# Differential queries and keys as three products of rounded halves, on one core

## The reference, cut to what matters

```python
xn = _rms(x, norm_mix_g)
z = jnp.einsum('btd,dc->btc', xn, w_in)
(m_qk, m_v, m_o, m_if, s_q, s_ckv, i_q, i_k, i_w, d_q, d_k, d_v, g_pre) = _split_cols(z)
...
y_b = _dsa(sq, sk, sv, iq, ik, i_w).reshape(B, T, S_WIDTH)
dq = _rope(_rms(d_q.reshape(B, T, DA_HEADS, 2, DA_HEAD_DIM), dq_g), cos, sin)
dk = _rope(_rms(d_k.reshape(B, T, DA_HEADS, 2, DA_HEAD_DIM), dk_g), cos, sin)
...
o = _diff_attn(dq, dk, dv, lam_val)
...
merged = (gates[:, :, 0] * jnp.einsum('btc,cd->btd', y_a, w_branch[0]) + ...
x = x + jnp.einsum('btd,de->bte', merged, w_out)
```

## Time and profile before

| | us |
|---|---|
| median of three runs | 2467.02 (2466.3 to 2468.4) |
| the profiled execution | 2466.4 |
| its span, first to last instruction | 2464.6 |
| TensorE busy | 2441.3 (99% of the span) |
| VectorE busy | 1851.7 (75%) |
| ScalarE busy | 1552.4 (63%) |

### The profile page before, as it was taken

How to read it: one execution, slowest core, us unless ns; L and a number is a source line. 1 busy time by engine, 2 the same in 40 slices (tenths; PEclk the granted TensorE clock), 3 DMA queues, 4 the chain that set the end, 5 groups by cost and what they waited for, 6 DMA issues and landing times.

```text
span 2464.6 us, 30527 instructions
## 1 busy us (share of the span) xinstructions
PE 2441.3 (99%) x12038; PEld 2037.7 (83%) x12038; DVE 1851.7 (75%) x1866; ACT 1552.4 (63%) x1896; POOL 111.3 (5%) x78
## 2 busy tenths in 40 slices
PE   9999999999999999999999999999999999999998
PEld 8788888897888888977888897888888888888886
DVE  7877744478786446645454479999999999999998
ACT  5666543367565444365443447788878787878886
POOL 0000000000000000010000002010101010101001
PEclk9999999999999999999999999999999999999999
DMA  7444555354336565677654556999999999999996
GB/s 260 145 154 154 208 190 181 117 186 153 132 137 212 199 212 171 204 258 261 250 188 176 166 197 265 395 369 380 374 373 380 373 377 367 381 366 390 358 383 249
DMA packets 185399, 634.31 MB, mean 257 GB/s; under 512 B 14324, under 2 KB 55668, under 8 KB 142089
## 3 DMA queue, kind: packets, MB, share of 16 engines
q1 hardware_dynamic: 175688, 608.21, 67.6%
q0 software_dynamic: 9536, 23.60, 2.5%
HBM read 616.56 MB, written 26.22 MB: 261 GB/s over the span
## 4 chain that ended last, share of the span: by engine, by line
PE 95%; DVE 3%; ACT 1%; issue 0%; DMA 0%; DVEq 0%; SPq 0%; ACTq 0%
PE bank L565 92%; PE bank L602 2%; PE bank L935 2%; DVE split L2210 1%; ACT split L1562 0%; DVE parts L2190 0%; PE bank L1483 0%; ACT parts L1562 0%; DVE oT_high L2224 0%; DVE x_resid L2252 0%; DMA const<-in_tables 0%; DVE xparts L2190 0%; DVE parts L2279 0%; DVE merged_low L2242 0%; DVE xs L2936 0%
## 5 line engine op out<-in xcount | busy, mean ns | idle before, releaser
L565 PE MATMUL bank<-split,parts 128*128 128x512 f32 (+1 forms) x6432 | 1465.7, 388 | 6.2 <-DVE split L2210 2.2
L565 PEld LDWEIGHTS bank<-split,parts 128*128 128x128 f32 x6432 | 1186.9, 188 | 251.7 <-issue 12.2
L1562 ACT ACTIVATE split<-ring 128x2048 fp32r<-128x2048 f32 x444 | 848.6, 1921 | 438.5 <-PE bank L565 437.8
L2210 DVE TENSOR_TENSOR split<-ring,split 128x2048 fp32r<-128x2048 f32 x444 | 993.7, 2284 | 45.8 <-ACT split L1562 45.5
L2279 DVE TENSOR_TENSOR parts<-bank,parts 128x512 fp32r<-128x512 f32 x128 | 82.5, 686 | 166.5 <-ACT parts L1562 165.8
L1562 ACT ACTIVATE halves<-ring 128x1024 fp32r<-128x1024 f32 x96 | 101.0, 1060 | 130.0 <-PE bank L565 129.6
L2224 DVE TENSOR_TENSOR halves<-ring,halves 128x1024 fp32r<-128x1024 f32 x96 | 116.2, 1224 | 73.0 <-ACT halves L1562 72.3
L565 PE MATMUL bank<-ring_low,z_high 128*128 128x512 f32 (+2 forms) x384 | 147.0, 383 | 0.0
L565 PE MATMUL bank<-xparts,halves 128*128 128x256 f32 x960 | 116.5, 283 | 0.2 <-DVE x_resid L2252 0.2
L565 PEld LDWEIGHTS bank<-xparts,halves 128*128 128x128 f32 x960 | 115.5, 192 | 0.8 <-DVE x_resid L2252 0.6
L565 PE MATMUL bank<-z_high 128*128 128x512 f32 (+3 forms) x304 | 111.2, 366 | 0.0
(11 more groups left out here) (349 smaller groups left out, 2411.9 us busy)
## 6 DMA issues: line engine op xcount, KB each, us to landing
ring<-in_moe_w_gate SPq DMA_DIRECT2D x112, 1024.0 KB, 7.7
ring<-in_moe_w_up SPq DMA_DIRECT2D x112, 1024.0 KB, 7.4
ring<-in_moe_w_down SPq DMA_DIRECT2D x112, 1024.0 KB, 7.6
ring<-in_w_gate_up SPq DMA_DIRECT2D x44, 1024.0 KB, 5.9
ring<-in_w_in SPq DMA_DIRECT2D x40, 1024.0 KB, 5.3
ring<-in_ret_w_in SPq DMA_DIRECT2D x24, 1024.0 KB, 5.3
ring<-in_w_down SPq DMA_DIRECT2D x22, 1024.0 KB, 6.8
ring<-in_w_in SPq DMA_DIRECT2D x20, 880.0 KB, 4.7
```

Of the source, the lines that this page charges most:

```text
L565: return nc.tensor.matmul(o, l, r, start=first, stop=final, **kw)
L1562: return nc.scalar.activation(out, in_, func, **kw)
L2210: V.tensor_tensor(split[:, split_place(m), 1, :], ring[:, n % RING, :], split[:, split_place(m), 0, :].bitcast(F32), ALU.subtract).then_in ...
```

## The change

In both layers of the first block:

- `dq` and `dk` are computed by `split_chunk`: their units get high parts (places B, A1 and A2, B) and low parts, and three rounded products take the place of one float32 product.
- In `split_chunk`, a unit that is not computed tile by tile starts when its high part is there: first the products with the weights' high part for both tiles (16), then a wait for the low part and the products with it (8).
- The inputs' second low part `xnT_low` and its signal are gone; all chunks use `xs_low`. `xnT` is free early, and `kv` and the merged branches live there; two places of the late half units swap.
- TensorE's order is `dq`, `dk`, the first unit of `dv`, the turning of the heads, the second unit of `dv`, the selected scores.
- ScalarE's and VectorE's orders are written anew around this: three of the new low parts stand inside `top_keys`, and the selected scores come after the rotation of the differential queries.

```diff
-COLUMNS = {"qk": "A1 A2", ... "kv": "A2", "dv": "A1 A2",
+COLUMNS = {"qk": "A1 A2", ... "kv": "A2", "dq": "B A1", "dk": "A2 B",
+           "dv": "A1 A2",
...
-            xnT_low = oT_high[:, KT:2 * KT, :].rearrange("p (t k) s -> p t k s", t=TT)
...
-        kv = xs
+        kv = xnT[:, :, :].rearrange("p (s k) t -> p s (k t)", s=TT)
+        merged = kv
...
+            def with_high(o, l, r, first):
+
+                mm(o, l(0), r(0), first, False)
+                mm(o, l(1), r(0), False, False)
+
+            def with_low(o, l, r, final):
+
+                return mm(o, l(0), r(1), False, final)
...
-                    w = take_column((4, n), chunk)
+                    w = take_column((4, n), chunk, column_low if u in by_tile else column_high)
+                    low = len(unit_of_column)
                     ins = []
-                    for tt in range(TT):
+                    if u not in by_tile:
+                        for part in range(2):
+                            if part:
+                                eng.wait_ge(column_low.sem, low)
+                            for tt in range(TT):
+                                c = slice(tt * P, (tt + 1) * P)
+                                for k in range(4 * u, 4 * u + 4):
+                                    l, r = (lambda i: mix_part(i, k)[:, c]), (lambda i: row(w[i], k % 4))
+                                    if part:
+                                        ins.append(with_low(bank[b[tt]][:, 0:n], l, r, k == KT - 1))
+                                    else:
+                                        with_high(bank[b[tt]][:, 0:n], l, r, k == 0 and bias is None)
+                    for tt in range(TT if u in by_tile else 0):
...
                 columns(z_dq, "dq")
-                tiles_dk = chunk_tiles(z_dk[1])
-                next(tiles_dk)
+                columns(z_dk, "dk")
+                units_dv = split_chunk(z_dv[1], "dv")
+                next(units_dv)
                 turn_heads(lambda tt, c: zc(tt, C_SQ + c, P), lambda tt, c: kv[:, tt, c:c + P])
...
-                next(tiles_dk)
-                next(tiles_dk, None)
-                point("dk")
+                for _ in units_dv:
+                    pass
+                point("dv")
                 head_scores(0)
...
-                eng.wait_ge(gate_in_low.sem, pe.next(gate_in_low))
-                low_in[0] = xnT_low
-                columns(z_dv, "dv")
...
+                column_highs("dq0")
                 z_evac(*z_o, ACT.Sigmoid)
-                column_highs("dv0")
+                column_highs("dq1")
                 for tt in range(TT):
                     for h in range(2):
                         copy(kv[:, tt, h * HALF:(h + 1) * HALF])
+                column_highs("dk0")
                 head_squares(lambda tt, h: kv[:, tt, h * HD:(h + 1) * HD], 8, lambda tt: kB + 8 * tt, in_yb)
+                column_highs("dk1")
+                z_evac(*z_dq)
+                column_highs("dv0")
                 roots(hsum[:, 2, kB:kY], hsum[:, 1, kB:kY])
+                head_squares(z_head(C_DQ), 8, lambda tt: kA + 25 * tt + 8, in_yb)
                 column_highs("dv1")
-                z_evac(*z_dq)
-                head_squares(z_head(C_DQ), 8, lambda tt: kA + 25 * tt + 8, in_yb)
+                z_evac(*z_dk)
+                head_squares(z_head(C_DK), 8, lambda tt: kA + 25 * tt + 16, in_yb)
+                turned_heads(0)
                 head_roots(8, 16)
-                z_tile(0, *z_dk)
-                turned_heads(0)
-                z_tile(1, *z_dk)
-                exps({2: ("g10",), 5: ("g11",)})
-                head_squares(z_head(C_DK), 8, lambda tt: kA + 25 * tt + 16, in_yb)
+                column_highs("g10")
                 z_evac(*z_dv)
+                exps({0: ("g11",)})
                 column_highs("g12")
...
-                column_lows("v0", "v1")
+                column_lows("v0", "v1", "o0")
                 head_mean_squares(z_heads(1, 0, 8), z_heads(0, 0, 8), HD)
-                column_lows("o0")
...
-                top_keys()
+                top_keys({(1, 0): ("dq0",), (1, 3): ("dq1",), (1, 6): ("dk0",)})
                 eng.wait_ge(act_freed.sem, dve.point("kv", act_freed))
                 V.memset(v_ext[:, :, :, M_DH:M_DH + 1], 1.0)
                 head_mean_squares(hsum[:, 1, kB:kY], hsum[:, 0, kB:kY], HD)
+                column_lows("dk1")
                 then(inverse_root(hsum, slice(kB, kY)))
                 for tt in range(TT):
+                    if tt:
+                        column_lows("dv0")
                     rope(kv[:, tt, 0:HALF], 8, tt, hsum[:, 3, kB + 8 * tt:kB + 8 * tt + 8], 1, done=rope_dve if tt else None)
-                column_lows("dv0", "dv1")
+                column_lows("dv1")
                 head_mean_squares(z_heads(1, 8, 16), z_heads(0, 8, 16), HD)
-                eng.wait_ge(for_act.sem, dve.point("dk", act_freed))
-                V.tensor_tensor(xnT_low, xnT[:, :, :].rearrange("p (t k) s -> p t k s", t=TT), xs_high.bitcast(F32),
-                                ALU.subtract).then_inc(gate_in_low.sem, gate_in_low.tick())
-                scores(lambda tt: msel[:, 0:P] if tt == 0 else msel[:, P:384])
-                column_lows("g10", "g11")
                 z_inverse(8, 16)
                 rope_from_z(C_DQ, 1)
+                column_lows("g10")
+                scores(lambda tt: msel[:, 0:P] if tt == 0 else msel[:, P:384], {2: ("g11",)})
                 head_mean_squares(z_heads(1, 16, 24), z_heads(0, 16, 24), HD)
```

More of the change, by code:

```diff
@@ L46 @@
 LAYER_HALVES = DEPTH * KT
-COLUMNS = {"qk": "A1 A2", "ckv": "B Y", "ix": "A1 A2", "sq": "B Y", "v": "A1 A2", "o": "B A1", "kv": "A2", "dv": "A1 A2",
+COLUMNS = {"qk": "A1 A2", "ckv": "B Y", "ix": "A1 A2", "sq": "B Y", "v": "A1 A2", "o": "B A1", "kv": "A2", "dq": "B A1", "dk": "A2 B",
+           "dv": "A1 A2",
            "g1": "E H A2 E", "b1": "A2 E", "g0": "H D A2 H", "g2": "A2 D E H", "b0": "G D", "b2": "H B"}
@@ L210, in build @@
             split = fx("split", [P, SPLITS, 2, UNIT])
-        late_halves = [oT_high[:, KT:2 * KT, :].rearrange("p k t -> p (k t)"), ybuf_tmp_high[:, 0:UNIT],
+        late_halves = [oT_high[:, 0:KT, :].rearrange("p k t -> p (k t)"), ybuf_tmp_high[:, 0:UNIT],
                        ybuf_tmp_high[:, 3 * 4 * SEQ:3 * 4 * SEQ + UNIT],
-                       oT_high[:, 0:KT, :].rearrange("p k t -> p (k t)")]
+                       oT_high[:, KT:2 * KT, :].rearrange("p k t -> p (k t)")]
         late_hidden = [oT_high[:, KT + 4 * i:KT + 4 * i + 4, :] for i in range(2)]
@@ L316, in build @@
         mix_high_made = signal("mixer_inputs_high")
-        gate_in_low = signal("gate_inputs_low")
         head_sums = signal("head_squares_summed")
@@ L513, in take_half, with take_column @@
                 return place_half(h, by_column)
-            def take_column(shape, chunk):
+            def take_column(shape, chunk, made=column_low):
                 n = issued[0]
@@ L524, in take_column @@
                 place_taken.append(name)
-                eng.wait_ge(column_low.sem, len(unit_of_column))
+                eng.wait_ge(made.sem, len(unit_of_column))
                 low = ring_low[:, n % RING, 0:k * width].rearrange("p (t c) -> p t c", t=TT)
@@ L1159, in turn_merged @@
                     eng.wait_ge(mrg_dve.sem, pe.next(mrg_dve))
-                    turn_input(xs, (2 * h, 2 * h + 1))
+                    turn_input(merged, (2 * h, 2 * h + 1))
                 def split_branch(br, ahead_of_last=None):
@@ L2510, in mlstm_outputs, with top_keys @@
                 ins.then_inc(yb_dve.sem, yb_dve.tick())
-            def top_keys():
+            def top_keys(between):
                 for tt in range(TT):
@@ L2534, in top_keys @@
                     for r in range(TOPK // 8):
+                        column_lows(*between.get((tt, r), ()))
                         src = acc if r == 0 else wk
@@ L2542, in top_keys, with scores @@
                     then(V.tensor_tensor(d, d, const[:, K_DIAG:K_DIAG + P], ALU.subtract))
-            def scores(mask):
+            def scores(mask, between={}):
                 for j in range(6):
+                    column_lows(*between.get(j, ()))
                     tt, ns, hs = score_bank(j)
@@ L2665, in merge @@
                             g = zc(tt, gate_column(br) + h * HALF, HALF)
-                            m = xs[:, tt, h * HALF:(h + 1) * HALF]
+                            m = merged[:, tt, h * HALF:(h + 1) * HALF]
                             if first:
```

## The result

The changed kernel takes 2470.74 us (median of 21 runs, 2469.35 to 2472.05), the kernel before 2467.02 in the same comparison (21 runs): ratio 1.0013, 95% interval 1.0007 to 1.0019. It is slower by 3.7 us. The forecast was 2466.2; the result lies inside the range and inside the 0.2% that I called no change, but on the other side of zero, and by more than its interval. The profiled execution has a span of 2468.2 us.

A forecast was written before the change was run, and what follows sets the result against it. TensorE, busy for 99% of the span, was taken as the bound. Of 4.53 us saved per layer the waits left some 0.4, 0.8 us in all, taking the median from 2467.0 to 2466.2; range 2459 to 2471.

The forecast's parts named there:

- What TensorE saves: Differential queries and keys: 96 rounded products (19.18 us) replace 32 float32 ones (23.71 us), 4.53 us less per layer.
- What the others get: Four more high parts on ScalarE; VectorE gets 5.3 us more per layer, selected scores ending at 145.4, not 135.00.
- The three waits: TensorE waits before turning the latents' keys and before the first and second products with selected probabilities: 0.8, 2.7, 0.7 us.
- From there on I find no further wait: Behind the second product with probabilities, the next copy and the fourth gate unit's low part are made before they are wanted.
- The slower clock: Rival: TensorE's clock falls after the long wait, 2.6 us lost per layer, 2471.4 in all; chance of a slower kernel 0.09.
- VectorE's sum sets the wait: VectorE's added-up order puts the scores 10 us later while TensorE comes 3.7 us earlier, so TensorE waits for probabilities.
- The rest costs nothing: Moved buffers, swapped places, SP and POOL queues, later hand-over of first tiles and interleaved low parts: counted as nothing.

The follow-up runs named there:

- the filled wait: Changed kernel with two products that nothing reads issued per layer while TensorE waits for the first copy of probabilities: 2466.84 us, ratio 0.9997.
- the six rounds: Changed kernel with six of eight rounds in the choice of keys (48 keys in place of 64): 2470.13 us, ratio 1.0009.
- The repair: Changed kernel with first two probability copies between the last exponentials, third gate unit's high part before the third group, sigmoids ahead of the root: 2460.12 us, ratio 0.9972.
- root first: Changed kernel with ScalarE making the root of the query sums ahead of its four copies of turned heads, all eight rounds: 2469.50 us, ratio 1.0010.
- sigmoids first: Changed kernel with the sigmoids of the third gate unit's bank ahead of the root of the differential keys' sums: 2468.14 us, ratio 1.0005.
- early copies: Changed kernel with the first two turned probabilities copied out between the groups of exponentials, after the fourth and sixth: 2468.94 us, ratio 1.0005.
- both kernels with low parts first: Every unit waits for its low part at its start: in the changed kernel 2473.17 us; in the kernel with early copies and early sigmoids 2467.22 us.
- six rounds, root first: Changed kernel with six of eight rounds in the choice of keys and the query sums' root ahead of the copies of turned heads: 2462.94 us, ratio 0.9980.
- copies and sigmoids early, low parts first: Kernel with early copies and early sigmoids (2460.12 us), but every unit waits for its low part at its start: 2467.22 us, ratio 0.9999.
- with the sigmoids first: Changed kernel with the bank's sigmoids ahead of the differential keys' root, plus two unread products in TensorE's wait: 2464.03 us, ratio 0.9987.

## Why the prediction was wrong, point by point

- *What TensorE saves* was right: 4.53 forecast, 4.48 measured. The Trainium skill ("FP8 and Floating Point Precision", TensorE Precision Notes) states four passes for true float32, from which the estimate of 5.9 for three passes came; the trace does not agree, and the measurement decides.
- *What the others get* was right within 0.8 us. VectorE's own rows, which answer to the earlier trace rows:

```profile
85.15 0.34 DVE L2548 TENSOR_SCALAR idx<-bank,iw 128x128 f32<-128x128 f32 x1
...
113.14 0.17 DVE L2118 TENSOR_SCALAR hsum<-hsum 128x16 f32<-128x16 f32 x1
...
126.14 0.26 DVE L2606 RECIPROCAL hsum<-hsum 128x16 f32<-128x16 f32 x1 [0.85 <-ACT hsum L1582]
...
134.58 0.68 DVE L2579 SCALAR_TENSOR_TENSOR pbuf<-bank,msel 128x512 f32<-128x512 f32 x1
```

  Forecast: 85.7, 113.7, 126.7, 135.3. Low parts inside the choice of keys took no more than their length.
- *The three waits* were right in place and a little too long: 0.8, 2.7 and 0.7 forecast, 0.30, 2.23 and 0.40 measured.
- *"From there on I find no further wait"* is a step that failed. I looked at the next copies and the next low part, but not at the bank that the next group of products writes to. Its row (149.53 in the trace of before) was not read: 2.5 us to spare, while TensorE was to come earlier and ScalarE later. In the first layer of the filled wait, where the clock holds, the third product stands 65.20 us behind the first key and value products, against 64.97 before: 0.2 us lost where the forecast had 0.4 saved. Against the forecast this step costs 0.6 us per layer, and only where the clock holds: in the changed kernel itself TensorE comes to the bank after it is free.
- *The slower clock* is the step that the result turns on. The sum puts it at nothing; it was a rival with 0.09, set aside because "the wait is shorter than the one at the start". A wait of 2.23 us was enough, once in the mixer of each layer. By the filled wait its price is 3.9 us for both layers, so most of the 4.5 us between forecast and result; the rival had 5.2, taken from a longer burst at the start. The reason given against it was wrong, though not every such wait brought a fall. The Trainium skill ("TensorE: Matmul & The Clock Gate", the table on why this matters) warns of idle gaps that bring the half clock back; the trace agrees in kind, with 0.5 behind the 2.23 us, but the gaps that the row names are longer than this wait, and the measurement decides.
- *VectorE's sum sets the wait* held in its number, since the sum had VectorE's wait for the root in it (1.0 us forecast, 0.85 measured). But it is half of the cause: the six rounds show that the chain through TensorE's turned heads and ScalarE's root is the later one, and less work on VectorE alone wins nothing.
- *Luck.* With the fall of the clock alone taken away the time was 2466.84, near the forecast 2466.2. The two agree because errors cancel: the three waits came out 1.27 us per layer shorter than forecast, and the small things below and the bank took that back.
- *The rest costs nothing* left out small things: up to the first product with probabilities, stages that should have kept their length are 0.70 us longer (the values' chunk 9.86 for 9.57, bias and first gate unit 6.11 for 6.01, turned probabilities 0.94 for 0.79, the 24 products behind them 5.79 for 5.63). Some 0.3 of it is how the ends count: the last product ahead of a wait takes 0.39 us to its end, where the next would have started 0.23 us behind it. Why the rest came was not tried.

The sum of these for the first layer: 4.48 - 2.53 (two waits) - 0.70 = 1.25 us earlier at the first product (1.79 less the 0.54 by which this execution started earlier), 0.61 at the second. Then 1.27 us are lost up to the bias (the bank alone would take 0.8 of it, slow products take 0.46 more) and 1.79 us to slow products up to the third, 2.45 late.

## What to carry to other kernels

When an edit makes the bound engine faster, list for the next dozen of its instructions everything each one needs, the bank it writes included, with the time it is free and the time it will now be wanted; the first with too little to spare is where the gain ends, and taking it away only leads to the next. A wait of 2 us in a dense stretch of products can cost about as much again through the clock, and may cost nothing more in the next layer. The repair lay in the order of the engine that releases, not in the products: moves on ScalarE that gave 1.2 to 2.6 us one at a time gave 10.6 together.

## What the runs showed of the hardware that was not expected

- The granted clock fell to 0.5 behind waits of 1.66, 2.2 to 2.3 and 3.1 us, for 6.83 or 3.41 us. It did not fall behind others of 1.66 us (second layer, root first), 2.23 us (second layer, sigmoids first) and 3.1 us (second layer, early copies), nor behind the 1.6 to 1.7 us of both kernels with low parts first. So the length of the wait alone does not decide, and the same code can lose 2 us in one layer and none in the next.
- It also fell for 3.41 us without a long wait nearby: at 634.9 (six rounds, root first) and 639.8 (copies and sigmoids early, low parts first), at 638.7 (sigmoids first, 20 us behind the wait), and at 621.64 in the filled wait. The kernel before seems to have this as well: of its 97 runs beside the experiments 53 show a mean clock of 0.999 and 2466.4 us on average, 38 show 0.998 and 2468.9, six 1.000 and 2466.9. How these mix in a group moves its median. No trace of a run of it at 0.998 is kept, so that the same falls lie behind it is not shown, and what makes them stays open.
- A filler of two float32 products in the wait kept the clock at 1.00 in the first layer of the filled wait and in both layers with the sigmoids first.
